# A decoder block that splits its weights once per group of rows: the split halves kept in DRAM and read back

## The reference

```
h = RMSNorm(x);  u = h @ w_in      # conv GLU 1024 | q 512 | k, v 64 | indexer q 512, k 64, weights 8 | gates 2048
branch A: GLU -> causal depthwise conv, 31 taps -> LayerNorm -> swish -> @ w_conv_out (512 x 1024)
branch B: the indexer scores all earlier keys of each row, the 256 best are kept, 8 heads attend to them
          with ALiBi distances -> @ w_attn_out (512 x 1024)
x = x + (sigmoid(gA) * A + sigmoid(gB) * B) @ w_out
x = x + (silu(n @ w_gate) * (n @ w_up)) @ w_down     # n = RMSNorm(x), inner width 2816
out = RMSNorm(x)
```

## Time and profile before

| | |
|---|---|
| median of three executions | 3765.64 us (3759.41 to 3768.01) |
| span of the profiled execution, first to last instruction | 3756.2 us; the page gives no other time for it |
| mean granted clock of PE | 0.955 of full speed |
| PE busy | 3311.2 us, 88% |
| PEld busy | 2693.5 us, 72% |
| DVE busy | 2509.2 us, 67% |
| ACT busy | 1563.5 us, 42% |
| POOL busy | 1559.3 us, 42% |
| data moved by DMA | 336.09 MB, 89 GB/s |

### The profile page before, as it was taken

How to read it: one execution, slowest core, us unless ns; L and a number is a source line. 1 busy time by engine, 2 the same in 40 slices (tenths; PEclk the granted TensorE clock), 3 DMA queues, 4 the chain that set the end, 5 groups by cost and what they waited for, 6 DMA issues and landing times.

```text
span 3756.2 us, 45382 instructions
## 1 busy us (share of the span) xinstructions
PE 3311.2 (88%) x15365; PEld 2693.5 (72%) x15365; DVE 2509.2 (67%) x4000; ACT 1563.5 (42%) x2755; POOL 1559.3 (42%) x830
## 2 busy tenths in 40 slices
PE   7961799799998899799998889978999878879998
PEld 6850688578887788568886777855788756768886
DVE  2958828778705838779996983877999989740001
ACT  3321553342334653263333665327333246733332
POOL 3420134226766144316665314431466622036666
PEclk9985899899999999899999999989999989999999
DMA  3420243233332243223332024322333210133332
GB/s 101 118 71 2 94 131 112 67 118 96 97 105 85 90 129 109 75 91 101 96 96 95 23 85 129 106 79 73 96 96 96 90 40 18 46 123 107 99 97 95
DMA packets 379748, 336.09 MB, mean 89 GB/s; under 512 B 9437, under 2 KB 345353, under 8 KB 377128
## 3 DMA queue, kind: packets, MB, share of 16 engines
q1 hardware_dynamic: 362688, 270.56, 23.8%
q10 hardware_dynamic: 16872, 63.01, 4.6%
HBM read 293.69 MB, written 39.85 MB: 89 GB/s over the span
## 4 chain that ended last, share of the span: by engine, by line
PE 49%; issue 28%; DVE 15%; POOL 4%; ACT 2%; DVEq 1%; DMA 1%; ACTq 0%; POOLq 0%
PE PS L1285 11%; PE PS L1256 10%; PE PS L1258 10%; PE PS L1257 10%; DVE flags L1059 2%; DVE W L931 2%; POOL WL L371 2%; DVE part_max L1146 1%; DVE W L1044 1%; DVE change L1085 1%; PE PS L1270 1%; PE PS L1272 1%; PE PS L1271 1%; PE PS L1246 1%; PE PS L1376 1%
## 5 line engine op out<-in xcount | busy, mean ns | idle before, releaser
L371 POOL TENSOR_TENSOR WL<-RAW,WH 128x1024 fp32r<-128x1024 f32 x464 | 1128.1, 2431 | 1725.6 <-ACT WH L512 1513.8
L512 ACT ACTIVATE WH<-RAW 128x1024 fp32r<-128x1024 f32 x464 | 490.9, 1058 | 1275.3 <-PE PS L1258 736.5
L1059 DVE TENSOR_SCALAR_CACHE_REDUCE flags<-W,cand 128x1408 uint8<-128x1408 f32 (+3 forms) x462 | 683.4, 1479 | 53.7 <-DVE cand L1089 40.0
L1256 PE MATMUL PS<-HF,WH 128*128 128x512 f32 x1408 | 550.1, 391 | 16.2 <-issue 13.8
L1257 PE MATMUL PS<-HF,WH 128*128 128x512 f32 x1408 | 549.5, 390 | 0.0
L1258 PE MATMUL PS<-HF,WL 128*128 128x512 f32 x1408 | 549.3, 390 | 0.0
L1285 PE MATMUL PS<-WH,HT 128*128 128x512 f32 x1920 | 519.2, 390 | 24.2 <-POOL WL L371 15.1
L1285 PEld LDWEIGHTS PS<-WH,HT 128*128 128x128 f32 x1920 | 360.5, 188 | 102.2 <-issue 16.6
L1256 PE MATMUL PS<-HT,WH 128*128 128x512 f32 x1088 | 428.3, 394 | 0.0
L1258 PE MATMUL PS<-HT,WL 128*128 128x512 f32 x1088 | 423.5, 389 | 0.0
L1257 PE MATMUL PS<-HT,WH 128*128 128x512 f32 x1088 | 423.4, 389 | 0.0
(11 more groups left out here) (193 smaller groups left out, 5433.8 us busy)
## 6 DMA issues: line engine op xcount, KB each, us to landing
RAW<-in_w_in SPq DMA_DIRECT2D x136, 512.0 KB, 3.8
RAW<-in_w_ffn_gate SPq DMA_DIRECT2D x88, 512.0 KB, 3.8
RAW<-in_w_ffn_up SPq DMA_DIRECT2D x88, 512.0 KB, 3.8
RAW<-in_w_ffn_down SPq DMA_DIRECT2D x88, 512.0 KB, 3.5
RAW<-in_w_out SPq DMA_DIRECT2D x32, 512.0 KB, 3.5
W<-in_x ACTq DMA_DIRECT2D x4, 2048.0 KB, 10.7
gate_b_scratch<-TMP ACTq DMA_DIRECT2D x32, 256.0 KB, 2.8
RAW<-in_w_conv_out SPq DMA_DIRECT2D x16, 512.0 KB, 3.4
```

The costliest lines, as they stand in the source:

```text
L371: nc.gpsimd.tensor_tensor(out=WL[:, slot, :], in0=RAW[:, slot, :], in1=WH[:, slot, :].bitcast(f32), op=ALU.subtract).then_inc(w_lo, 1)
L512: nc.scalar.activation(WH[:, slot, :], RAW[:, slot, :], ACT.Copy).then_inc(w_hi, 1)
L1059: step(nc.vector.tensor_scalar(flags[:, 0:n], SC[:, t, 0:n], cand[:, t:t + 1].bitcast(f32), 0.0, op, ALU.add, accum_out=count[:, t:t + 1]))
L1256: mm(PS[:, bank, :], wh, src[:, 0, k, :], start=k == 0, stop=False)
```

## The change

The chunks of group 0 (A0, C0, F0: 116, called fresh) are loaded and split as before, and each pair of halves is also stored to a DRAM scratch (1 MB a chunk). Every other chunk (348) is loaded from there, both halves in one DMA of 1 MB, and is neither copied by ACT nor subtracted by POOL. WH and WL become one tile WS (two slots of both halves), and a third slot W3 lies over RAW; fresh chunks use two slots, the others three. Where stages of both kinds meet, the loads wait for the place to be free. The store of chunk c-2 is issued by SP ahead of the load of c, and `hi` of chunk c now also waits until the store of c-2, out of the same slot, has landed. Loops over chunks on SP, PE and (for fresh stages) POOL are written out.

```diff
+    KEPT = sum(LEN.values())
+    PHASE_OF = [ph for ph in ORDER for _ in range(LEN[ph[0]])]
+    FRESH = [g == 0 for _, g in PHASE_OF]
+    NTH_FRESH = [sum(FRESH[:c]) for c in range(TOTAL)]
+    SLOT = [(c - BASE[PHASE_OF[c]]) % (2 if FRESH[c] else 3) for c in range(TOTAL)]
+    LANDING = [sum(not FRESH[b] and SLOT[b] == SLOT[c] for b in range(c)) for c in range(TOTAL)]
...
+    kept_dram = nc.dram_tensor("split_weights_scratch", (KEPT, P, 2, 1024), f32, kind="Internal").ap()
...
-        WH = sb("WH", [P, 2, 1024], f32r)
-        WL = sb("WL", [P, 2, 1024], f32r)
-        RAW = sb("RAW", [P, 2, 1024], f32)
+        WS = sb("WS", [P, 2, 2, 1024], f32r)
+        RAW, W3 = region(("RAW", [P, 2, 1024], f32), ("W3", [P, 2, 1024], f32r))
...
+            return (WS[:, s - 2, 1, :] if g == 0 else W3[:, s - 2, :])[:, part * 512:part * 512 + w]
...
+            def keep(c):
+                sp.wait_ge(w_lo, NTH_FRESH[c] + 1)
+                ph, g = PHASE_OF[c]
+                sp.dma_start(kept_dram[PLACE[ph] + c - BASE[ph, g]], WS[:, SLOT[c], :, :].bitcast(f32)).then_inc(w_kept[SLOT[c]], 16)
...
             def load(c, slot, dst, src):
-                if not isinstance(c, int) or c >= 2:
-                    sp.wait_ge(w_lo, c - 1)
-                sp.dma_start(dst, src).then_inc(w_in_slot[slot], 16)
+                ph, g = PHASE_OF[c]
+                n = NTH_FRESH[c]
+                if FRESH[c]:
+                    if c > BASE[ph, g] + 1:
+                        keep(c - 2)
+                    elif before(c, 2) >= 0:
+                        sp.wait_ge(w_used, before(c, 2) + 1)
+                    sp.dma_start(dst, src).then_inc(w_in_slot[slot], 16)
+                    return
...
+                s = SLOT[c]
+                last = before(c, s)
+                if last >= 0:
+                    sp.wait_ge(w_used, last + 1)
+                if s < 2 and FRESH[last]:
+                    sp.wait_ge(w_kept[s], 8 * n)
+                elif s == 2 and (last < 0 or FRESH[c - 3]):
+                    sp.wait_ge(w_lo, n)
+                if ph == "C" and c == BASE[ph, g] + 2:
+                    sp.wait_ge(pt_used, pt_end(g, PAIRS - 1))
+                to = W3[:, :, :] if s == 2 else WS[:, s, :, :]
+                sp.dma_start(to.bitcast(f32), kept_dram[PLACE[ph] + c - BASE[ph, g]]).then_inc(w_landed[s], 16)
...
             def lo(c, slot):
-                pool.wait_ge(w_hi, c + 1)
+                if not FRESH[c]:
+                    return
+                pool.wait_ge(w_hi, NTH_FRESH[c] + 1)
...
             def hi(c, slot):
-                if isinstance(c, int) and c >= TOTAL:
+                if c >= TOTAL or not FRESH[c]:
                     return
+                n = NTH_FRESH[c]
+                act.wait_ge(w_in_slot[slot], 16 * (n // 2 + 1))
+                if n >= 2:
+                    act.wait_ge(w_used, before(c, slot) + 1)
+                    act.wait_ge(w_kept[slot], 16 * (n // 2))
+                nc.scalar.activation(WS[:, slot, 0, :], RAW[:, slot, :], ACT.Copy).then_inc(w_hi, 1)
...
+            def arrived(c):
+                if FRESH[c]:
+                    pe.wait_ge(w_lo, NTH_FRESH[c] + 1)
+                else:
+                    pe.wait_ge(w_landed[SLOT[c]], 16 * (LANDING[c] + 1))
```

More of the change, by code:

```diff
@@ L75, in build_block, with before @@
         assert LEN[ph[0]] % 2 == 0
+    PLACE = {"A": 0, "C": LEN["A"], "F": LEN["A"] + LEN["C"]}
+    KEPT = sum(LEN.values())
[4 more added lines that the diff above has]
+    LANDING = [sum(not FRESH[b] and SLOT[b] == SLOT[c] for b in range(c)) for c in range(TOTAL)]
+    def before(c, slot):
+        return max((b for b in range(c) if SLOT[b] == slot and (slot < 2 or not FRESH[b])), default=-1)
     def blocks(g):
@@ L309, in _ @@
                     for col, at in ((COL_GB, A_GB), (COL_GA, A_GA)):
[L310 to L315, removed]
+                        for j in range(KD):
+                            load(c0 + at + j, j % 2, cols(j % 2, KD), win_v[:, :, col + P * j:col + P * (j + 1)])
+                    for j in range(N_CO):
+                        load(c0 + A_CO + j, j % 2, cols(j % 2, KC), wco_v[:, :, 2 * P * j:2 * P * (j + 1)])
+                    last_keeps(ph, g)
                 elif ph == "C":
@@ L328, in _ @@
                             sp.dma_start(MA[:, :, :], ma_dram[g]).then_inc(gm_in, 16)
-                    with sp.Fori(0, KD // 2) as i:
-                        for u in range(2):
-                            load(c0 + KC + u + 2 * i, u, cols(u, 1), wout_v[:, ds(u + 2 * i, 1), :])
+                    for j in range(KD):
+                        load(c0 + KC + j, j % 2, cols(j % 2, 1), wout_v[:, j:j + 1, :])
+                    last_keeps(ph, g)
                 else:
@@ L1254, in col_chunk @@
                         pe.wait_ge(ready, ready_at + k + 1)
-                    wh, wl = WH[:, slot, k * P:(k + 1) * P], WL[:, slot, k * P:(k + 1) * P]
+                    wh, wl = (split(c, part)[:, k * P:(k + 1) * P] for part in range(2))
                     mm(PS[:, bank, :], wh, src[:, 0, k, :], start=k == 0, stop=False)
@@ L1269, in half_chunk, with row_chunk @@
                         o = PS[:, banks[e], :]
[L1270 to L1272 removed]
+                        mm(o, split(c, 0)[:, at], src(0, k), start=k == 0, stop=False)
+                        mm(o, split(c, 0)[:, at], src(1, k), start=False, stop=False)
+                        ins = mm(o, split(c, 1)[:, at], src(0, k), start=False, stop=k == KC - 1)
                 ins.then_inc(w_used, 1)
[L1275 to L1277 removed]
+            def row_chunk(c, src, k, first, last, order, row_done=None, held_by=None):
+                arrived(c)
                 for t in order:
[L1279 to L1280 removed]
+                    if held_by is not None and t in held_by:
+                        pe.wait_ge(*held_by[t])
                     for part in range(2):
                         lhs = src[:, part, k, t * P:(t + 1) * P]
[L1283 removed]
+                        for w_part in range(2 - part):
                             for half in range(2):
[L1285 to L1286 removed]
+                                ins = mm(PS[:, 2 * t + half, :], lhs, split(c, w_part)[:, half * 512:(half + 1) * 512],
+                                         start=first and part == 0 and w_part == 0, stop=last and part == 1)
                     if row_done is not None and t != order[-1]:
```

104 lines of the change are left out of this document (49 added, 55 removed).

## The result

The changed kernel takes 3663.8 us (median of 4 runs, 3662.0 to 3665.6) beside 3762.5 us (3758.8 to 3768.0) for the kernel before: a ratio of 0.9738, interval [0.9724, 0.9752], 98.7 us less. Forecast were 81.5 us less, at 3684 us.

A forecast was written before the change was run, and what follows sets the result against it. F stages are bound by TensorE; elsewhere GpSimd's weight split slows VectorE, and TensorE waits. Gains of 106.5 us less 25 us for stores gave -81.5 us, 3684 us; likeliest 3665 to 3705, full range 3650 to 3745 us.

The forecast's parts named there:

- Rival 1: Fresh chunks in A0, C0, F0: storing them costs nothing and C3's start runs at full clock; 3657 us; chance 0.17.
- A1 to A3: wait for the convolution: VectorE's taps, freed of GpSimd's subtraction, end earlier, so TensorE's wait goes entirely: 20.1 us a stage.
- A1 to A3: mean's matmuls at full clock: TensorE doesn't stop before the mean, so its matmuls run like the variance's: 2.9 us a stage.
- A1 to A3: layer norm's tail: One product of the tail sat behind a GpSimd subtraction: about 1.8 us of 7.2 us gained per stage.
- weight parts of C1 to C3: TensorE's waits behind the split, 2.3 us and 1.2 us, shrink: 3 us a stage, 9 us.
- F1 to C2: GpSimd's last sums, no longer paced by TensorE, let F1 end like F0: 4.1 us gained.
- F2 to C3: The 11.37 us wait at F2's end surely goes; C3's start gains 0 to 8.7 us; 19 us taken together.
- fresh path and its handover: Stores of 1 MB ahead of loads in A0, C0, F0: 0.2 us a chunk, 25 us with the handover to A1.
- Rival 4: VectorE's convolution taps are not freed, 60 us of the gains don't come: 3744 us; chance 0.04.
- rival 5: In F2 the search stays in step with GpSimd's operations, so C3's wait stays: 3692 us; chance 0.12.
- Rivals 2 and 3: Fresh path costly: store and load one after the other, 3735 us, chance 0.18; or the case of rival 3.
- rival 3: Slower than before: the store bounds A0, C0 and F0, with a 13.3 us loop; 3799 us; chance 0.10.

The follow-up runs named there:

- e8: Kernel before, GpSimd's subtraction in A1 to A3 replaced by a memset of 64 columns that reads nothing from SBUF: 3691.0 us, ratio 0.9803.
- e9: Changed kernel with GpSimd kept busy in A1 to A3, two unneeded 512-column subtractions after each of the first 32 chunks: 3705.0 us, ratio 0.9847.
- e5: Changed kernel with GpSimd's product, low half and sums in F2 over 32 of 512 columns: 3655.0 us, ratio 0.9712.
- e1: Kernel before, with GpSimd's subtraction in A1 to A3 over 64 of 1024 columns: 3801.6 us, ratio 1.010.
- e3: Changed kernel, stores of all but two fresh chunks cut to 128 KB, later loads taken from the first two stored chunks: 3660.7 us, ratio 0.9724.
- e2: Changed kernel with every store of group 0 made twice, once to a spare scratch: 3829.4 us, ratio 1.0158.
- e4: Changed kernel, loads of F1's and F2's second and third chunk held until stage A's convolution stores have landed: 3652.2 us, ratio 0.9711.

## Why the prediction was right, and where its terms were not

The mechanism was right and the time lay in the range, but 20 us under the forecast of 3684 us and just below the 3665 to 3705 us that had the largest chance. Rival 1, to which I had given 0.17, came nearest with 3657 us: the fresh path was nearly free. The sum, by its own terms, in the us of the profiled executions:

| term | forecast | measured | from |
|---|---|---|---|
| A1 to A3: wait for the convolution | -60.4 | -60.4 | waits 80.4 to 20.0 |
| A1 to A3: mean's matmuls at full clock | -8.7 | -8.7 | 6.49 to 3.59 |
| A1 to A3: layer norm's tail | -5.4 | -6.0 | 7.2 to 5.2 |
| weight parts of C1 to C3 | -9 | -20.8 | table of stretches |
| F1 to C2 | -4 | -6.7 | the same |
| F2 to C3 | -19 | -15.7 | the same |
| indexer in A1 to A3 | 0 | +18.2 | mean to F, less the two rows above |
| fresh path and its handover | +25 | +6.4 | A0, C0, F0 |
| sum | -81.5 | -93.7 | span: -93.6 |

**VectorE freed: right.** The wait and the mean's matmuls came out as worked out, and e8 and e9 show the cause from both sides. Rival 4 falls. One reading was off: a tap is recorded with some 740 ns, but in a run of them the next starts 0.66 us after it (37.21 us for 56), so 88 taps needed 58.5 us and GpSimd had cost them 29.5 us a stage, not 22.6. The forecast took only the 20.1 us that TensorE waited, so this did not change it.

**Weight parts of C: mis-sized, 9 us for 20.8.** I had read only two of the rows. TensorE's waits for L1194 (9.1 us in four before, 2.3 in one after), for L1185 (10.7 to 6.4) and for the subtraction (1.2 us each in C1 and C2, gone) fell by 13.5 us. The stretches also hold the attention ahead of the weight part, whose many short waits fell by 3.6 us. For the other 3 to 4 us I have no row of their own; before, the granted clock was 0.50 for 3.4 us where the weight parts of C1 and C3 begin (from 1292.4 and 3292.6), and after it was not, which would be a reason that is only argued. The row for L1185 was in the same list of waits as those I used.

**The end of F2: rival 5 happened in part.** The sure 11.37 us went, with about 2 us of the slow-clock restart behind it. Of the 8.7 us of C3's wait only 2.4 came. The term that fell short was the search's gain: it had to end some 16 us earlier in its stage and ended 13.0 us earlier (335.3 us after F2's start instead of 348.4), which did little more than make up for F2's own earlier end. I had counted some 12 turns of 1 us in the row chunks and 6 to 8 us elsewhere. 10 turns took 9.9 us (2 before), in and behind the row chunks; in the column chunks GpSimd's busy time was no measure, but where its operations lie. They recur every two chunks, 10.88 us; a turn freed of them takes 9.9 to 10.0; so a turn that comes earlier meets the next operation, is held to its end, and goes on at 10.88, as 16 turns did. This was the mechanism that the Trainium skill's rule gives ("SBUF — State Buffer", Who interferes with whom), and e5 shows it by taking the operations' length away. e1 and e8 agree with the same rule: up to 28.2 us for the 64 columns that are read, 0.15 us for those that are only written.

**The fresh path: mis-sized, 25 us for 6.4 (by stretches) or 3 (by e3).** A store of 1 MB landed 5.0 us after its issue, and the load, issued 0.4 us behind it, 6.3 us after its own, so 6.7 us where I had 0.3 + 2.9 + 3.8 = 7.0 us for the two. The loop is then 6.7 + 3.5 = 10.2 us, inside 10.88, and F0 is full. The estimate from the Trainium skill ("DMA: Bandwidth & Descriptors", Anatomy of one DMA), 4.4 us for such a store, is nearer to 5.0 than the queue's data time of 2.9 (the page gives its fit for DMAs that GpSimd issues, here SyncE does); either fits into the loop. My 0.2 us a chunk was a margin, not a reading: the loop I had worked out fitted by 0.3 us, and F0, whose loop fits, lost 0.3 us in 66 chunks (table of stretches). Rivals 2 and 3 fall; e2 shows that rival 3's point exists. Of the 6.4 us, 2.0 are the start: the first load of x, beside the first stores of weights, landed after 13.7 us instead of 12.0.

**Missed: the convolution's stores.** I let 1 MB loads "cost nothing" with the argument that they have two chunks' time. That was true of the loads and says nothing of what they do to others. The place in the trace of before was the issue rows of the 256 KB stores and the row of VectorE waiting for them, 2.3 us, and the share of DMA time, 0.33 in F0 with 101 GB/s, which the change would double. TensorE's waits for L728 in A1, A2 and A3 rose from 2.3 to 17.0 us, and the two spells at clock 0.50 at the ends of the long ones cost a few us more (an estimate: TensorE was busy for 5.4 and 5.1 us in them, and half of that is 5 us). e4 gives 11.7 back.

So the terms were off by 12 and 3 us (more gained), 3 and 18 us (less gained) and 19 us (less paid), and partly cancelled: the sum missed by 12 us, and that it missed by no more is luck. Between the medians it is 17 us, since the profiled execution of before lay further under its median than that of after. The other 3 us up to 3684 are the median of before itself, 3765.6 us in three executions and 3762.5 in four. The range had to carry the fresh path, whose ends I had set from nothing to 233 us.

## What to carry to other kernels

Read which engine is held, not which is busy: moving an off-path GpSimd operation out of a stage of two-input VectorE work was worth some 24 us a stage where TensorE waited for VectorE (73 us in three, e8), and nothing in F3, which took 374.1 us before and after. When a change raises the bytes moved, look in the trace for every small transfer that somebody waits for, and order the large ones behind it; a loop of transfers that fits into the time of its matmuls is hidden whole, and one that doesn't is paid in full, so work out whether it fits and add no margin a chunk. A periodic helper and a search loop with nearly the same period can lock to each other, and busy shares don't show it. When a stage gets shorter, what runs beside it has to get shorter by as much before any wait at its end falls.

## What the runs showed of the hardware that I had not expected

- GpSimd can be starved: 64 columns, 0.31 us at least, took up to 28.2 us beside back-to-back taps of VectorE (e1), while a write of the same columns took 0.15 us (e8). Shortening an operation made the kernel 39 us slower.
- The search ran at 10.88 us a turn in 16 of F2's 30 turns, beside GpSimd operations of only 1.3 us, and at 9.9 to 10.0 us in all of them without (e5).
- Stores of 256 KB on ScalarE's queue went from 2.1 to 5.3 us (median, issue to landing), and the last ones of a stage to 9.9 us, when 1 MB loads ran on SP's queue. Over a whole stage the DMA engines were only some 55% taken (F1), but 98% in the 13 us in which A2's last stores were under way (changed kernel, from 1573). With two loads held back the wait for them fell from 25.1 to 11.9 us (e4).
- DMA engines 89% taken, 285 GB/s, cost F0 next to nothing (0.3 us more than before from its first matmul to C1's first scores); at 1.01, 379 GB/s, each chunk took 1.3 us more (e2).
